# The decay differences of a chunked DeltaNet: a matmul over transposed gates in place of operands made by GpSimd

## The reference, cut to what matters

```python
def chunk_gated_delta(q, k, v, g, beta):   # g = log of the gate, per token and head
    ...
    gc = jnp.cumsum(g, axis=-1)
    diff = gc[..., :, None] - gc[..., None, :]
    decay = jnp.exp(jnp.where(incl, diff, -jnp.inf))     # incl: lower triangle
    kb = k * beta[..., None]
    a_low = jnp.where(strict, jnp.einsum("bhnid,bhnjd->bhnij", kb, k) * decay, 0.0)
    lower = a_low + jnp.eye(c)
    sol = triangular_solve(lower, rhs, ...)
    attn = jnp.einsum("bhnid,bhnjd->bhnij", q, k) * decay
    ...
```

## Time and profile before

| | us |
|---|---|
| median of three runs | 2427.94 |
| lowest, highest | 2427.25, 2431.07 |
| profiled execution, its own time | 2431.82 |
| its span | 2430.0 |

### The profile page before, as it was taken

The page is one execution under the profiler, slowest core; times in us unless marked ns, Lnnn a source line. Parts: engine busy times, 40 slices in busy tenths (PEclk is TensorE's granted clock), DMA queues, the critical chain, the costliest instruction groups (busy, mean ns, idle before and its releaser), DMA issues.

```text
span 2430.0 us, 37480 instructions
## 1 busy us (share of the span) xinstructions
PE 2367.1 (97%) x12069; PEld 2001.3 (82%) x12069; DVE 1560.0 (64%) x2481; ACT 1246.1 (51%) x2205; POOL 168.3 (7%) x123
## 2 busy tenths in 40 slices
PE   8999998998999999999999999999999999999998
PEld 6787886886778888888888888888888888888886
DVE  5567768758767676556765555565677555676654
ACT  5556545535535554444554455554555444555544
POOL 0010102102100010000100000000001000010000
PEclk9999999999999999999999999999999999999999
DMA  6565344344236665666666657566666666666555
GB/s 231 161 171 164 110 115 146 106 129 139 62 104 178 186 185 192 194 192 186 186 185 194 193 184 217 141 184 191 195 189 189 192 193 194 185 185 185 193 193 173
DMA packets 230431, 418.88 MB, mean 172 GB/s; under 512 B 27276, under 2 KB 31261, under 8 KB 230173
## 3 DMA queue, kind: packets, MB, share of 16 engines
q1 hardware_dynamic: 230301, 417.14, 56.9%
HBM read 414.94 MB, written 2.10 MB: 172 GB/s over the span
## 4 chain that ended last, share of the span: by engine, by line
PE 89%; issue 5%; DVE 3%; POOL 1%; DMA 1%; ACT 1%; SPq 0%; DVEq 0%; POOLq 0%; ACTq 0%
PE pair L477 17%; PE pair L478 17%; PE pair L479 17%; PE pair L496 10%; PE aux L496 10%; PE aux L498 5%; PE pair L498 5%; PE aux L667 4%; PE aux L525 3%; DVE w_lo L1454 1%; DVE r L1655 1%; POOL state_out L2105 0%; PE aux L706 0%; POOL Y L2102 0%; DMA raw<-in_tok_w_out 0%
## 5 line engine op out<-in xcount | busy, mean ns | idle before, releaser
L1454 DVE TENSOR_TENSOR w_lo<-raw,w_hi 128x512 fp32r<-128x512 f32 x1536 | 1093.8, 737 | 617.2 <-ACT w_hi L984 612.2
L984 ACT ACTIVATE w_hi<-raw 128x512 fp32r<-128x512 f32 x1536 | 939.4, 633 | 778.8 <-DMA raw<-in_ffn_w 622.4
L477 PE MATMUL pair<-w_hi,xT 128*128 128x512 f32 x960 | 390.8, 407 | 23.6 <-DVE w_lo L1454 16.0
L477 PE MATMUL pair<-w_hi,hid_hi 128*128 128x512 f32 x1012 | 394.3, 390 | 0.0
L479 PE MATMUL pair<-w_hi,hid_lo 128*128 128x512 f32 x1012 | 393.8, 389 | 0.0
L478 PE MATMUL pair<-w_lo,hid_hi 128*128 128x512 f32 x1012 | 393.7, 389 | 0.0
L479 PE MATMUL pair<-w_hi,xT 128*128 128x512 f32 x960 | 378.1, 394 | 0.0
L478 PE MATMUL pair<-w_lo,xT 128*128 128x512 f32 x960 | 377.8, 394 | 0.0
L496 PE MATMUL pair<-xT,w_hi 128*128 128x512 f32 x1024 | 362.3, 398 | 0.4 <-DVE h L1920 0.2
L496 PE MATMUL aux<-xT,w_hi 128*128 128x512 f32 x1024 | 360.8, 397 | 0.0
L498 PE MATMUL aux<-xT,w_lo 128*128 128x256 f32 x1024 | 287.4, 281 | 0.0
(11 more groups left out here) (236 smaller groups left out, 1632.7 us busy)
## 6 DMA issues: line engine op xcount, KB each, us to landing
raw<-in_ffn_w SPq DMA_DIRECT2D x1024, 256.0 KB, 3.1
raw<-in_dn_w_in SPq DMA_DIRECT2D x208, 256.0 KB, 2.8
raw<-in_tok_w_out SPq DMA_DIRECT2D x128, 256.0 KB, 3.1
raw<-in_gm_w_in SPq DMA_DIRECT2D x112, 256.0 KB, 2.9
raw<-in_mem_w_kv SPq DMA_DIRECT2D x64, 256.0 KB, 2.8
h<-in_x SPq DMA_DIRECT2D x4, 1024.0 KB, 7.6
r<-in_mem SPq DMA_DIRECT2D x2, 1024.0 KB, 7.1
h<-in_mem_columns SPq DMA_DIRECT2D x2, 1024.0 KB, 6.3
```

The source lines that it names most:

```text
L477: pe.matmul(acc, act_hi[:, kt, tokens], w_hi[:, slot], start=start, stop=False)
L984: act.activation(w_hi[:, slot], raw[:, slot], ACT.Copy).then_inc(hi_ready, 1)
L1454: dve.tensor_tensor(w_lo[:, slot], raw[:, slot], w_hi[:, slot].bitcast(F32), ALU.subtract).then_inc(tiles_split, 1)
```

## The change

The cumulated gates of a group, 16 columns (2 chunks x 2 directions x 4 heads) of 128 tokens, are put into `gc_wide` by GpSimd: as they are in columns 0 to 15, negated in columns 32 to 47, zeros elsewhere. TensorE transposes them once (new bank number DGC, put between DA and DD, so that each later number up to DFT grows by one). A new VectorE function, `decay_rows`, spreads the transposed rows: `gc_rows` is 16 x (4 x 128) with each row kept in its own head's block only, `gc_minus` is 16 x (4 x 128) with the negated rows, one block for each f. The other rows of these two hold constant ones and zeros, set once by GpSimd before the first group. One matmul for each f then gives the difference of the cumulated gates for four heads, and VectorE subtracts the constant 1e30 mask from it. To keep the count of bank numbers, the transposition at the end of the ladder (DFT) uses three banks in place of four. Of the diff, all that the execution sees:

```diff
-STAGE = 22528
+STAGE = 22784
-C_ALL = C_LEV + len(LEVELS) * HALF
+C_DH = C_LEV + len(LEVELS) * HALF
+C_DF = C_DH + 4
+C_ALL = C_DF + 60
@@ shape_constants
+    for first in (0, 32):
+        for r in range(16):
+            m, d, hh = r // 8, r // 4 % 2, r % 4
+            c[first + r, C_DH + hh] = 1.0
+            c[first + r, C_DF + 2 * d + m] = 1.0
@@
-DA, DD, DE, DF, DG, DH, DI = 0, 6, 10, 14, 18, 22, 26
+DA, DGC, DD, DE, DF, DG, DH, DI = 0, 6, 7, 11, 15, 19, 23, 27
-DWV = DFT + 4
+DWV = DFT + 3
@@ buffers
+        gc_wide = sb(dn, "gc_wide", [P, P])
-        g_up = Y[:].rearrange("p d (b h) i -> p (d b) h i", b=2)
-        g_big = state_out[:].rearrange("p a b (h i) -> p (a b) h i", h=4)
+        gc_rows = Y[:, 1, 0:4, :]
+        gc_minus = Y[:, 1, 4:8, :]
@@ TensorE, deltanet
+                pe.wait_ge(sem("gate_columns"), g * 2 + 2)
+                transposes(base + DGC, [(0, gc_wide[:])], rnd)
                 by_tokens(0, DD)
...
                 for f in range(4):
                     fill(DF + f)
-                    pe.wait_ge(sem("decay_operands"), g * 8 + (2 * f + 1))
-                    done(pe.matmul(bank(DF + f)[:], ones, g_up[:, f].rearrange("p h i -> p (h i)"),
+                    have(DGC)
+                    done(pe.matmul(bank(DF + f)[:], gc_minus[:, f, :], gc_rows.rearrange("p h i -> p (h i)"),
                                    start=True, stop=True), DF + f)
...
-                for m in range(2):
-                    for hp in range(2):
-                        transposes(base + DFT + 2 * m + hp,
-                                   [(k * P, XL[:, 0, m, 2 * hp + k, :]) for k in range(2)], rnd)
+                transposes(base + DFT, [(k * P, XL[:, 0, 0, k, :]) for k in range(4)], rnd)
+                for hp in range(2):
+                    transposes(base + DFT + 1 + hp, [(k * P, XL[:, 0, 1, 2 * hp + k, :]) for k in range(2)], rnd)
+                for m in range(2):
+                    have(DV + m)
                 yield
                 have(level_aux(len(LEVELS) - 1, 1, "XY"))
-                for n in range(4):
+                for n in range(3):
                     have(DFT + n)
-                for m in range(2):
-                    have(DV + m)
@@ ScalarE: the copies of DFT, one of 4 heads and two of 2 instead of four of 2
@@ VectorE, deltanet
+                def decay_rows():
+                    fil(DGC)
+                    spread = lambda part: bank(DGC)[part, 0:P].unsqueeze(1).broadcast_to([16, 4, P])
+                    wide = lambda c, part: cst[part, c:c + 4].unsqueeze(2).broadcast_to([16, 4, P])
+                    top, low = slice(0, 16), slice(32, 48)
+                    dve.tensor_tensor(gc_rows[top], spread(top), wide(C_DH, top), ALU.mult).then_inc(sem("decay_half"), 1)
+                    free(dve.tensor_tensor(gc_minus[low], spread(low), wide(C_DF, low), ALU.mult), DGC)
...
                 convolve(2, 0)
                 yield
+                decay_rows()
                 square_sums(1)
                 yield
...
-                    dve.wait_ge(sem("decay_operands"), g * 8 + (2 * f + 2))
-                    free(dve.tensor_tensor(NT[:, f // 2, f % 2], heads(DF + f), g_big[:, f], ALU.subtract), DF + f)
+                    c = (C_BIGF, C_BIGB)[f // 2]
+                    free(dve.tensor_tensor(NT[:, f // 2, f % 2], heads(DF + f), over(cst[:, c:c + P], 4), ALU.subtract), DF + f)
@@ GpSimd, deltanet
-                for f in range(4):
-                    decay_operands(f)
+                gc = gs[:, 2 * G_GC:2 * G_GC + 4, :].rearrange("p r h -> p (r h)")
+                pool.tensor_tensor(gc_wide[:, 0:16], gc, zeros[:, 0:16], ALU.add).then_inc(sem("gate_columns"), 1)
+                pool.tensor_tensor(gc_wide[:, 32:48], zeros[:, 0:16], gc, ALU.subtract).then_inc(sem("gate_columns"), 1)
@@ GpSimd, once, before the first group
+            pool.memset(gc_wide[:], 0.0).then_inc(sem("gate_rows_cleared"), 1)
+            pool.memset(Y[:, 1], 0.0).then_inc(sem("gate_rows_cleared"), 1)
+            pool.wait_ge(sem("consts_loaded"), 16)
+            pool.wait_ge(sem("gate_rows_cleared"), 2)
+            wide = lambda c: cst[:, c:c + 4].unsqueeze(2).broadcast_to([P, 4, P])
+            pool.tensor_copy(gc_rows[32:48], wide(C_DH)[32:48]).then_inc(sem("gate_rows_cleared"), 1)
+            pool.tensor_copy(gc_minus[0:16], wide(C_DF)[0:16]).then_inc(sem("gate_rows_cleared"), 1)
+            pool.wait_ge(sem("gate_rows_cleared"), 4)
```

More of the change, by code:

```diff
@@ L1196, in deltanet @@
                     free(act.activation(NT[:, 1, m].rearrange("p h i -> p (h i)"), bank(n)[:], ACT.Copy), n)
+                for n in range(4):
+                    drained(act, base + DG + n, rnd)
                 for m in range(2):
-                    drained(act, base + DG + 2 * m, rnd)
-                    drained(act, base + DG + 2 * m + 1, rnd)
                     drained(act, base + DH + 2 + m, rnd)
@@ L1230, in deltanet @@
                     yield
-                for m in range(2):
[L1232 to L1236, removed]
+                fil(DFT)
+                free(act.activation(XT0[:, 0], by_head(bank(DFT)[:]), ACT.Copy), DFT)
+                for hp in range(2):
+                    n = DFT + 1 + hp
+                    fil(n)
+                    free(act.activation(XT0[:, 1, 2 * hp:2 * hp + 2, :],
+                                        bank(n)[:, 0:2 * P].rearrange("p (h i) -> p h i", h=2), ACT.Copy), n)
                 yield
@@ L2096, in deltanet @@
                 flat = lambda t: t.rearrange("p m h -> p (m h)")
[L2098 to L2106, removed]
                 for c in (0, 2 + SEQ):
```

## The result

The changed kernel takes 2440.97 us (median of 8 runs, 2434.52 to 2445.75), the kernel before 2428.89 us in the runs beside it (8 runs, 2427.25 to 2431.07). The ratio is 1.0049, 95% interval 1.0041 to 1.0058: slower by 0.49%, about 12 us. The forecast was 2435.3 us, in a range that ended at 2440.5.

A forecast was written before the change was run, and what follows sets the result against it. TensorE, busy 97%, was taken to bound the kernel, with VectorE late at the groups' heads. Three stalls 3 x 3.5 + 0.3 for transposes - 3.4 for GpSimd's release = +7.4 us, giving 2435.3 us, range 2430.5 to 2440.5.

The forecast's parts named there:

- What bounds the kernel; what GpSimd costs: Second group's head: GpSimd's wide operands slow VectorE, which TensorE awaits; releasing them takes 3.4 us off, bounds 0 to 4.4.
- rival A: TensorE's second k transposes: no stall, only -3.1 us, 2424.8 us, or 2421.4 with the third group's splits; chance 0.09.
- The added work off the stall: Extra transposes cost 0.3 us in all; decay matmuls, GpSimd's constants, mask and ladder's end 0; VectorE's two products 1.28 us.
- The stall: Second four k transposes (DD+3) wait until VectorE drains DGC: 3.6 us in first group, 3.3 in third; 3.5 taken each.
- The clock: Behind each stall: old low stretch falls into the stall, another like it follows, 2.3 us on the slab; net 0.
- rival B: Each stall brings one more, equally long low clock stretch costing 1.7 us: +12.5 us, 2440.4 us; chance 0.12.
- The base: Profiled execution before stood 3.9 us above the median 2427.94; the same difference was applied to the forecast, giving 2435.3 us.
- The range: Whole kernel: 2430.5 to 2440.5 us, resting on stalls of 2.0 to 5.2 us and a gain of 0 to 4.4.

The follow-up runs named there:

- late_number: Changed kernel with DGC numbered and transposed behind DD and decay_rows run behind square_sums(1); 2425.65 us, ratio 0.9990 to the kernel before.
- late_again: The same kernel as late_number, run again in the second series; 2425.14 us, ratio 0.9991 to the kernel before.
- before_memset: Kernel before with each group's eight wide GpSimd operands replaced by memsets to zero, leaving the decay matrices out; 2426.07 us, ratio 0.9989.
- early_drain: Changed kernel with VectorE's decay_rows moved right behind the last k tap, bank numbers kept; 2424.49 us, ratio 0.9984 to the kernel before.
- busy_stall: Changed kernel with the first four k transposes made seven times, keeping TensorE at work while it waits; 2435.09 us, ratio 1.0029 to the kernel before.
- before_stalled: Kernel before with one added wait: TensorE's second four k transposes wait for VectorE's first reduction of square_sums(1); 2439.19 us, ratio 1.0046.
- mid_drain: Changed kernel with decay_rows moved behind the two splits after the last k tap, ahead of the v taps; 2429.50 us, ratio 1.0003.

## Why the prediction was wrong

- **What bounds the kernel; what GpSimd costs.** Right. VectorE was late at the head of the second group because of GpSimd. Without the operands and without the stall the gain is 2 to 4 us of time by the ratios (late_number, late_again, before_memset, early_drain), where rival A had -3.4 + 0.3 = -3.1. The term itself holds: from the second projection's transposes to those of the silu'd k the second group fell from 29.3 to 25.6 us in late_number and 25.8 in late_again. Up to the normalised k it fell by 5.0 us, more than 3.4, as the low stretch there then ran ahead of the wait for silu(1), where TensorE would have waited for VectorE anyway (that wait is 0.9 us in late_number, 2.5 before). (A's other figure has a slip of 0.1: -3.1 - 3.3 gives 2421.5, not 2421.4.)
- **The added work off the stall.** Right: no cost of the transpose, the bank shift, the ladder's end or the constants shows. late_number (0.9990) is level with before_memset (0.9989), which has GpSimd's release without the added work. The two products took 1.38 us, 1.28 was assumed, and are hidden wherever nobody waits for them.
- **The stall.** Mechanism, place and length right: DD+3 waits for DGC, 3.12, 3.09 and 3.54 us, against 3.6, 3.6 and 3.3; the first four transposes took part of the 3.6 us. ScalarE's second square came 3.3 us behind its first. The engines behind did not make it longer.
- **The clock: the step that failed.** The prediction said "Net 0" for it and counted 3.5 us a group. The whole effect of the stall is 14 us (late_number and early_drain against the changed kernel), 4.8 us a group. Of that, 9.75 us are the waits, 3.25 a group, and nearly 5 us go when TensorE is kept busy in them (busy_stall): some 1.5 us a group on average. I had the low stretch of before fall into the stall, which it did, and one more of the same length behind it. What came in the first group was low from 226.8 to 237.0, 10.2 us, with 5.3 us of it over the slab instead of 2.3; the second group has the same length. In the third the low clock rose only from 3.4 to 6.8 us. One low stretch there ran ahead of the wait for the SiLU, which shrank from 2.40 to 1.00 us, so that the distance grew by 3.8 us for a wait of 3.54. So rival B's mechanism took place in two groups of three. Its price of 1.7 us a group was near the average of 1.5, partly by luck, since the groups differ; its chance of 0.12 was too small. In the sum, 3 x 4.8 - 3.1 = +11.3 us gives 2440 us on the runs beside the result.
- **The base.** The profiled execution of before stood 3.9 us above its median, which I took as an offset common to both. 3 us of it come from one stretch of the MLP, which no other profiled execution has. This moved no term, but it hid them: the spans differ by 7.9 us, near the forecast's 7.4, while at 746 against 757 the kernels are 11.0 us apart and the medians 12.1.
- **The range.** Its end at 2440.5 took B's terms without any spread of the medians; the kernel before itself read 1 us higher in the later runs.

## What to carry to other kernels

- When results share banks by number, a new number is a new wait: look up who asked for that bank next, and where the reader of the new result stands in its own queue. Here one line, moved over four splits and four taps on VectorE, turned +10 us into -4.
- A wait of 3 us on TensorE behind another one cost on average about 1.5 us more than its length, through the clock, but not everywhere: 0.2 us more in the third group, and next to nothing in the profiled execution of before_stalled. Look at the granted clock behind a wait, and at whether TensorE works or waits there, before the wait is priced by its length. Waits of 0.3 to 0.8 us can be dear too: mid_drain lost 5 us at the median to 1.8 us of them.
- Two executions can differ by 3 us in a stretch that no edit touched. Follow the offset between two traces along the program instead of comparing spans.

## What was not expected of the hardware

The first half of the first MLP ran at two paces in two executions of the same instructions. TensorE's matmuls there, first the kernel before from 785 to 925, then the changed kernel from 796 to 936, which is the same work 11 us later (busy, mean ns of one):

```profile
L496 PE MATMUL aux<-xT,w_hi 128*128 128x512 f32 x192 | 68.0, 399 | 0.0
L498 PE MATMUL aux<-xT,w_lo 128*128 128x256 f32 x192 | 53.9, 281 | 0.0
```

```profile
L504 PE MATMUL aux<-xT,w_hi 128*128 128x512 f32 x192 | 66.7, 391 | 0.0
L506 PE MATMUL aux<-xT,w_lo 128*128 128x256 f32 x192 | 53.8, 280 | 0.0
```

399 against 391 ns, at a full clock and with no wait in either. It adds up to 3.0 us between the first and the last of eight blocks, and all the other profiled executions went at the quick pace. What sets it stays open.

A low clock cost nothing where TensorE would have waited anyway. In early_drain's and late_number's first group the low stretch came earlier (about 222 to 226), and the wait for silu(1) shrank from 2.46 to 1.24 and 1.28 us. late_again is the same kernel as late_number; there the stretch came behind the wait, which was 2.48 us, and the distance was 36.7 instead of 35.1 us. Where the low stretch falls is thus worth over 1 us in a group, which may be part of the several us by which runs of one kernel differ.
